# A single-core transformer kernel whose SBUF tiles start at byte 0 of a 512-byte line instead of byte 128, while the split weight slots stay at byte 128

## What is computed

```
block 1:  h = rmsnorm(x);  proj = h @ w_in
          oa = dilated_attention(...)   (12 heads, three dilations)
          ob = banded_attention(...)    (8 query heads, window 128, sinks)
          mix = sigmoid(ga)*(oa @ w_branch_a) + sigmoid(gb)*(ob @ w_branch_b)
          x = x + mix @ w_out
          x = x + square(relu(rmsnorm(x) @ w_up)) @ w_down      (width 4096)
block 2, layers 0 and 1:
          x = x + 0.5 * swiglu(rmsnorm(x), wi, wo)              (width 1408)
          stick-breaking attention, chunked mLSTM, latent attention, from one projection
          x = x + (g0*(sb @ up_sb) + g1*(ml @ up_ml) + g2*(mla @ up_mla)) @ w_out
          x = x + 0.5 * swiglu(rmsnorm(x), wi, wo)
```

## Time and profile before

| | |
|---|---|
| median of three executions | 2405.95 us |
| span of the profiled execution, first to last instruction | 2406.4 us |
| TensorE busy with matmuls | 2379.8 us, 99% |
| TensorE busy with weight loads | 1924.6 us, 80% |
| VectorE / ScalarE / GpSimd busy | 1209.2 / 965.8 / 1316.2 us |
| granted TensorE clock, mean | 0.998 of full |
| DMA moved | 213.40 MB, 89 GB/s over the span |

### The profile page before, as it was taken

How to read it: one execution, slowest core, us unless ns; L and a number is a source line. 1 busy time by engine, 2 the same in 40 slices (tenths; PEclk the granted TensorE clock), 3 DMA queues, 4 the chain that set the end, 5 groups by cost and what they waited for, 6 DMA issues and landing times.

```text
span 2406.4 us, 29717 instructions
## 1 busy us (share of the span) xinstructions
PE 2379.8 (99%) x11108; PEld 1924.6 (80%) x11108; DVE 1209.2 (50%) x1961; ACT 965.8 (40%) x1513; POOL 1316.2 (55%) x1589
## 2 busy tenths in 40 slices
PE   8999999999999999999999999999999999999999
PEld 8777778888888888777787888888887777788887
DVE  5997765423224432379625743333325785266331
ACT  4554444322223223566524432332336764344321
POOL 5763246656556655366244765555554562466554
PEclk9999999999999999999999999999999999999999
DMA  5321123333333333222122333333332221223333
GB/s 166 109 71 53 47 77 97 96 97 97 97 97 110 97 97 103 71 72 69 54 87 79 97 97 97 96 97 97 97 98 67 72 78 53 88 87 98 96 97 96
DMA packets 59758, 213.40 MB, mean 89 GB/s; under 512 B 6624, under 2 KB 6752, under 8 KB 59488
## 3 DMA queue, kind: packets, MB, share of 16 engines
q1 hardware_dynamic: 59472, 211.38, 29.2%
q10 hardware_dynamic: 144, 0.14, 0.0%
HBM read 209.39 MB, written 2.10 MB: 88 GB/s over the span
## 4 chain that ended last, share of the span: by engine, by line
PE 91%; DVE 6%; issue 1%; ACT 1%; DMA 0%; POOL 0%; SPq 0%; DVEq 0%; ACTq 0%
PE banks L721 89%; DVE t L1203 1%; DVE t L1211 1%; DVE t L1213 1%; DVE t L1488 1%; DVE t L1204 1%; DVE t L1197 1%; DVE t L1219 0%; PE banks L841 0%; PE banks L995 0%; DVE t L1222 0%; ACT t L1679 0%; DMA t<-in_w 0%; PE banks L875 0%; POOL t L1992 0%
## 5 line engine op out<-in xcount | busy, mean ns | idle before, releaser
L721 PE MATMUL banks<-t,t 128*128 128x512 f32 (+4 forms) x10788 | 2351.7, 387 | 17.2 <-ACT t L1699 5.9
L721 PEld LDWEIGHTS banks<-t,t 128*128 128x128 f32 (+2 forms) x10788 | 1889.5, 188 | 452.2 <-issue 64.3
L1992 POOL TENSOR_TENSOR t<-t,t 128x256 fp32r<-128x256 f32 x1544 | 1258.9, 846 | 1049.9 <-ACT t L1679 1041.5
L1679 ACT ACTIVATE t<-t 128x1024 fp32r<-128x1024 f32 x385 | 408.2, 1060 | 1078.8 <-issue 605.5
L1197 DVE TENSOR_TENSOR t<-banks,t 128x512 f32<-128x512 f32 x121 | 83.1, 687 | 169.8 <-PE banks L721 169.2
L1378 DVE TENSOR_TENSOR t<-banks,t 128x512 f32<-128x512 f32 x44 | 30.4, 690 | 184.5 <-PE banks L721 184.3
L1346 DVE SCALAR_TENSOR_TENSOR t<-banks,t 128x512 f32<-128x512 f32 x32 | 22.1, 691 | 155.4 <-PE banks L721 155.4
L1080 DVE SCALAR_TENSOR_TENSOR t<-t,t,t 128x512 fp32r<-128x512 f32 x64 | 52.0, 817 | 58.1 <-ACT t L1699 58.1
L1323 DVE TENSOR_TENSOR t<-t,t 128x512 fp32r<-128x512 f32 x68 | 70.5, 1036 | 2.3
L1352 DVE TENSOR_TENSOR t<-banks,t 128x512 f32<-128x512 f32 x24 | 16.6, 691 | 106.0 <-PE banks L721 106.0
L1699 ACT ACTIVATE t<-t,t 128x512 fp32r<-128x512 f32 x64 | 45.6, 715 | 55.7 <-DVE t L1346 49.1
(11 more groups left out here) (182 smaller groups left out, 1304.7 us busy)
## 6 DMA issues: line engine op xcount, KB each, us to landing
t<-in_w SPq DMA_DIRECT2D x386, 512.0 KB, 3.5
t<-in_xT SPq DMA_DIRECT2D x8, 256.0 KB, 5.7
out<-t SPq DMA_DIRECT2D x8, 256.0 KB, 4.5
t<-in_dmask SPq DMA_DIRECT2D x1, 1536.0 KB, 7.7
t<-in_vbias SPq DMA_DIRECT2D x2, 384.0 KB, 4.1
t<-in_c SPq DMA_DIRECT2D x1, 576.0 KB, 8.6
t<-in_w SPq DMA_DIRECT2D x2, 256.0 KB, 3.9
t<-in_pos SPq DMA_DIRECT2D x2, 256.0 KB, 4.1
```

Source lines behind the costliest of these rows:

```text
L721: return pe.matmul(o, l, r, start=start, stop=stop, skip_group_check=True)
L1679: a.activation(whl[u % 2][:, 0:1024], wraw[u % 3][:, :], ACT.Copy).then_inc(*w_high.next(u))
L1992: p.tensor_tensor(hl[:, 1024:2048][:, c], wraw[u % 3][:, c], as_f32(hl[:, c]), ALU.subtract).then_inc(*w_low.next((u, q)))
```

## The change

Three things are changed in the layout, and nothing in the instructions.

- `base` is rounded up to a multiple of 512 in place of 64: it becomes 16,896, which is 33 x 512.
- Between the raw slots and the split slots stand now `turn_t` (64 bytes) and 64 bytes of nothing, so both `whl` slots begin at byte 128 of a line. Behind them stand `rcol_t` (32 bytes) and 352 bytes of nothing, so all that follows begins at byte 0 again.
- Behind the region `turn_t` and `rcol_t` are gone; `cols_t` loses seven spare elements and goes last, behind `small_t`. So `mask_r`, `vb_t` and `small_t` begin at byte 0 of a line, and `cols_t` at byte 448.

```diff
-        base = -(-nc.sbuf_base // 64) * 64
+        base = -(-nc.sbuf_base // 512) * 512
...
         wraw = [take(1024) for _ in range(3)]
+        turn_t = take(16)
+        top[0] += 64
         whl = [take(2048, F32R) for _ in range(2)]
+        rcol_t = take(8)
+        top[0] += 352
         tab = take(2 * S)
...
         R0 = top[0]
         top[0] += 110 * KB
-        turn_t = take(16)
         mask_r = take(512, F32R)
         later_r = {"ntri": mask_r[:, 256:384], "nones": mask_r[:, 384:512]}
         vb_t = take(768)
-        rcol_t = take(8)
-        cols_t = take(NCOL + 7)
         small_t = take(112)
+        cols_t = take(NCOL)
```

## The result

The changed kernel takes 2450.28 us, the median of four runs (2448.69 to 2451.48). The kernel before took 2406.89 us beside it, median of four. The ratio is 1.0178, with a 95% interval of 1.0166 to 1.0191, so about 43 us more. I had put 2406 us first and 2365 to 2440 us as the range: the time lies above it, and near rival B's "at most 2457 us".

What follows compares the result with a forecast made beforehand. TensorE was taken to bound the kernel, through the number of matmuls times their 226.7 ns pitch. Every term was taken as 0, summing to 0 on the profiled 2406.4 us: forecast 2406 us, range 2365 to 2440 us.

Steps and rivals of the forecast that it cites:

- rival B: Every 512-column matmul: the new distance makes the weight load collide, at most +51 us, 2457 us; 0.08 in full, 0.14 in part.
- What bounds the kernel: TensorE, busy 2379.8 of 2406.4 us: the time is, to a few per cent, the number of matmuls times their pitch.
- Activation tiles against weight halves: All 9204 512-column matmuls: tiles at byte 0, halves at 128, both at 128 before; bounds -123 to +51 us, taken 0.
- no change: Whole kernel: likeliest case, pitch stays at 226.7 ns and time within a few microseconds, 2401 to 2411 us; chance 0.50.
- The price from the nearest rows: Matmuls behind a piece of attention: a state about 5.5 ns worse; over 9204 matmuls +51 us, the upper bound.
- Raw slots, other tiles, small tables: Accesses outside the big matmuls' operands: loads ±0.4 us, VectorE and ScalarE operands 3.4 us, `mask_r` 1 us either way; each taken 0.
- Rival A: 512-column matmuls: the extra is a collision that 128 bytes remove, -96 us, 2310 us; 0.12 in full, 0.10 in part.
- the two conditions: Rival B, dense matmuls: a loss over 39 ns on the weight load, outlasting the previous columns, or a slower moving stream.
- Rival C: Some of about 3500 matmuls outside smooth stretches: the state behind attention gets shorter, -5 us, 2401 us; chance 0.06.

## Why the prediction was wrong, step by step

**What bounds the kernel: right.** The time is the number of matmuls times the pitch. The chain has the same two pieces with the same counts, and 46.2 us more of TensorE's busy time explain the 43.1 us more of span.

**Activation tiles against weight halves: the step that failed.** I bounded it at -123 to +51 us and took 0, since the pitch "looks like a fixed step between a weight load and a matmul rather than a collision of reads". It measured +43 us, by the change and by moving the halves alone. There is no such fixed step: at a granted clock of 0.50 the same matmuls stand at 426.7 ns, the columns alone, and this was in the trace of the kernel before. The reading error was this: the rows showed a pitch that was the same over many addresses, and I took that for independence of the address. But all those addresses were the same modulo 256, and by the runs that is the part that counts. A constant in a trace in which the one relevant quantity never varies says nothing about it. I had noted just that, and still put half of the chance on "no change".

**The price from the nearest rows: near, in part by luck.** The rows behind a piece of attention gave a state 5.5 ns worse, which I used as the upper end: +51 us. The changed kernel's long stretches stand at 232.3 ns, 5.6 ns more. Fewer matmuls pay it in full than the 9204 of the sum, as those behind attention paid already: 43 us. The run with one slot displaced suggests why the two are alike. It comes back to 226.7 ns by 236, 228, 233 and 231 ns, and by the starts of the single records the matmuls behind the piece of attention in the earlier trace rows come back by these same four lengths. So after either disturbance TensorE needs some matmuls to settle, and at a distance of 128 bytes it never does; that is my reading and no run isolates it. But nothing in the working tied 5.5 ns to 128 bytes: at 192 bytes the price is 2.1 ns, at 96 bytes 7.5.

**Raw slots, other tiles, small tables: right at 0.** The run with the raw slots alone (0.9998) and that with everything at byte 0 (1.0002) show it.

**Rival A, faster: not seen.** None of the seven distances tried gives 512-column matmuls under 226.7 ns. Its argument keeps a grain: 256-column matmuls reach 113.5 ns, and at the lower clock the whole extra is gone, as it would be if reads got in each other's way.

**Rival B, slower: the case that happened.** Its place was right and its price near. Of the two conditions that I gave it, the first was not met: the weight load does not outlast the columns. The loads stay at 188 ns in the records, as before, and 861 x 188 ns are 162 us of 200. The loss comes with the load ending in good time, which leaves the second, a slower moving stream, or a later handover to the next matmul. Rival B had 0.08 in full; a distance between two streams that read at once, which the trace had never shown, deserved as much as "no change".

**Rival C, a small gain behind attention: not seen.** Of the 43.1 us more of span the two long pieces hold 23.0; the other 20 us fall on the rest of the kernel, where the attention work is.

**The range** left out this case on purpose, by 0.08. With it inside, the upper end would have been some 2457 us.

## What to carry to other kernels

When matmuls follow each other without a gap, each with its own weight load, put the weights and the moving tile at the same place modulo 256 bytes. Here, with 512 columns in the `F32R` format, a shift of 32 bytes cost 2%; no run shows another format, and the few matmuls of 256 columns did not lose. A layout edit can be judged by one number: the count of matmuls in a fixed, unbroken stretch at full clock. And if every row of a trace agrees in a quantity, the trace has no evidence on what another value would do: give the bounds the weight, not the middle. First look for a quantity that does vary: here a few stretches at the lower clock already showed that the extra was no fixed step.

## What was not expected of the hardware

- The distance counts, and 256 bytes are as good as none: 0 and 256 give 226.7 ns, 128 gives 232.3, 96 gives 234.2, and 192 gives 228.8 (200 us by the count in each run).
- Off the good distances the pitch runs through short cycles, 231 and 235 ns by turns at 32 bytes. At 128 bytes one kernel shows two of them in different stretches, seven matmuls from 228 to 241 ns, and 230 and 237 by turns.
- At a granted clock of 0.50 the pitch is 426.7 ns, the 512 columns alone, at distance 0 and at 128; at 1.00 the same matmuls take 13.4 and 19.0 ns more than their 213.3.
- Halving one weight load of three, and with it the width of that matmul, made the 512-column matmuls longer, 871 for 882 in 200 us at a clock of 1.00.
